# Two-block transformer kernel on one core: order and buffers of the modulation vectors in the first stages

## The reference, cut to what matters

```
h = rms_norm(x, g_mix)                       # x is 1024 tokens x 1024
z = h @ w_in                                 # iq (256), ik (64), iw (4), cx, cy (512 each), gt (3*1024), ...
q_i = rope(iq)   # 4 heads of 64;   k_i = rope(rms_norm(ik, g_idx_k))
w_i = iw * (IDX_HEADS ** -0.5 * IDX_DIM ** -0.5)
dots  = einsum('bqhe,bse->bqhs', q_i, k_i)   # per block of 128 queries
score = einsum('bqhs,bqh->bqs', relu(dots), w_i)
_, idx = lax.top_k(score, 256)               # which keys the second branch may see
gates = sigmoid(gt + b_gate)
# second block, once for each of its two layers and two conditions
mod = silu(cond) @ w_ada + b_ada             # w_ada is 1024 x 3072: shift, scale, gate
```

## Time and profile before

| | |
|---|---|
| median of three runs | 4141.89 us |
| the profiled execution's own time | 4143.85 us |
| its span | 4142.0 us |
| TensorE matmul busy | 3646.8 us (88%) |
| VectorE busy | 2171.8 us (52%) |
| ScalarE busy | 1415.1 us (34%) |
| mean DMA rate | 56 GB/s |

### The profile page before, as it was taken

One profiled execution on the slowest core, in us unless ns is written; L12 is line 12 of the kernel. 1 busy time (PEld: TensorE's weight loads), 2 busy tenths in 40 slices (PEclk: granted clock), 3 DMA queues, 4 the chain that ended last, 5 costly groups with the idle time before them and its releaser, 6 DMA issues. The chain is left out here.

```text
span 4142.0 us, 46440 instructions
## 1 busy us (share of the span) xinstructions
PE 3646.8 (88%) x19222; PEld 3017.1 (73%) x19222; DVE 2171.8 (52%) x3943; ACT 1415.1 (34%) x2519; POOL 238.0 (6%) x343
## 2 busy tenths in 40 slices
PE   7999988886999999999898788888698888888788
PEld 5888866765778888788666576776586777776667
DVE  4599934555733322323555545555535656425563
ACT  3211344444122211112344434444424445424341
POOL 2012110000100000000000000000000000000000
PEclk9799999887999999999899998988798999989999
DMA  3223330002421111111210001000211000100112
GB/s 122 83 104 126 117 108 27 21 21 81 163 82 46 46 38 51 53 47 36 87 34 23 29 26 32 26 27 22 91 61 65 31 30 30 36 20 18 32 33 95
DMA packets 69572, 230.08 MB, mean 56 GB/s; under 512 B 8745, under 2 KB 12841, under 8 KB 69361
## 3 DMA queue, kind: packets, MB, share of 16 engines
q1 hardware_dynamic: 43056, 132.68, 9.8%
q0 software_dynamic: 22848, 81.85, 5.8%
q10 hardware_dynamic: 3456, 12.58, 0.8%
HBM read 180.42 MB, written 36.17 MB: 52 GB/s over the span
## 5 line engine op out<-in xcount | busy, mean ns | idle before, releaser
L2388 PE MATMUL PS<-m,m 128*128 128x512 f32 (+3 forms) x3560 | 1419.7, 400 | 151.1 <-DVE m L2737 35.3
L2390 PE MATMUL PS<-m,m 128*128 128x512 f32 (+3 forms) x3560 | 1380.0, 389 | 0.0
L2389 PE MATMUL PS<-m,m 128*128 128x512 f32 (+3 forms) x3560 | 1379.3, 389 | 0.0
L2388 PEld LDWEIGHTS PS<-m,m 128*128 128x128 f32 (+2 forms) x3560 | 688.9, 194 | 327.5 <-issue 65.4
L2390 PEld LDWEIGHTS PS<-m,m 128*128 128x128 f32 (+2 forms) x3560 | 688.6, 194 | 137.7 <-issue 1.2
L2389 PEld LDWEIGHTS PS<-m,m 128*128 128x128 f32 (+2 forms) x3560 | 692.0, 195 | 120.2 <-issue 2.1
L2734 DVE TENSOR_TENSOR m<-m,m 128x1024 fp32r<-128x1024 f32 (+5 forms) x204 | 211.7, 1038 | 422.0 <-ACT m L2572 421.3
L3020 DVE TENSOR_TENSOR m<-PS,m 128x512 fp32r<-128x512 f32 x352 | 240.9, 689 | 295.3 <-ACT m L2664 295.0
L2664 ACT CAST m<-PS 128x512 fp32r<-128x512 f32 x352 | 205.4, 589 | 495.1 <-PE PS L2494 493.8
L2485 PE MATMUL PS<-m,m 64*128 64x256 f32 (+5 forms) x1968 | 254.1, 369 | 70.3 <-ACT m L2653 53.8
L2485 PEld LDWEIGHTS PS<-m,m 64*128 64x128 f32 (+1 forms) x1968 | 214.9, 199 | 115.0 <-ACT m L2653 69.0
(11 more groups left out here) (196 smaller groups left out, 3894.4 us busy)
## 6 DMA issues: line engine op xcount, KB each, us to landing
m<-in_w SPq DMA_DIRECT2D x220, 512.0 KB, 3.5
g_scratch<-m ACTq DMA_DIRECT2D x24, 512.0 KB, 2.6
m<-g_scratch POOLq DMA_DIRECT2D x24, 512.0 KB, 4.5
m<-in_w SPq DMA_DIRECT2D x32, 256.0 KB, 2.5
x_scratch<-m POOLq DMA_DIRECT2D x2, 4096.0 KB, 12.9
m<-m POOLq DMA_DIRECT2D x60, 128.0 KB, 2.7
m<-in_xT POOLq DMA_DIRECT2D x24, 256.0 KB, 7.4
y_scratch<-m POOLq DMA_DIRECT2D x12, 512.0 KB, 3.0
```

The source lines that it names most:

```text
L2388: pe.e.engine.matmul(o, L[0], X[0], start=start, stop=False)
L2389: pe.e.engine.matmul(o, L[0], X[1], start=False, stop=False)
L2390: return pe.e.engine.matmul(o, L[1], X[0], start=False, stop=stop)
```

## The change

Five things are written in another order, and nothing is added to or taken from the arithmetic.

- In `ik` two modulations stand instead of three, each behind three k-steps.
- The column sums of the second norm come two k-steps before the end of `iq0`'s first half, and their spreading after two k-steps of `iq1` instead of four, so that six k-steps of `iq1` stand behind it.
- The loads of weight tiles 3 and 4 (`cx0`, `cy0`) are issued before the first modulations' loads. They were issued behind the first five of those.
- From the second norm's end on the ring has four buffers instead of two: the two of the beginning and two further ones, and within the scores four others that lie over temporary buffers no longer in use. In the gate stage it has two again. There are four signals instead of two.
- Between `iq1` and the scores stand eight modulations instead of five, and twelve between the scores instead of eight, one behind every second head. The last six gates (18 to 23) have none. The total stays 48.

```diff
-MOVES, GATE_STORES, RING = 12, 4, 2
+MOVES, GATE_STORES, RING = 12, 4, 4
...
+    def m_use(slots, upto, after=()):
+
+        n = len(m_slots)
+        m_ring.update(slots=slots, start=n, upto=min(upto, 48), after=list(after))
+        m_fetch(n + len(slots))
+
+    def m_fetch(upto):
+        slots, start = m_ring["slots"], m_ring["start"]
+        while len(m_slots) < min(upto, m_ring["upto"]):
...
+            m_slots.append(slots[(n - start) % len(slots)])
+            free = m_ring["after"] + [(S.mod, m_all[n - RING])] * (n >= RING) if n - start < len(slots) else [
+                (S.mod, m_all[n - len(slots)])]
...
-    m_fetch(RING, [t_x[7, 0]])
+    w_load(5)
+    m_use(first_ring, 2, [t_x[7, 0]])
...
-            for _ in range(3):
-                steps_of(ik, 2)
+            for _ in range(2):
+                steps_of(ik, 3)
                 modulate()
             steps_of(ik, 2)
-            steps_of(q0, 8)
+            steps_of(q0, 6)
             next(second)
-            steps_of(q1, 4)
+            steps_of(q0, 2)
+            steps_of(q1, 2)
             finish(second)
             normed = [t for k in range(8) for t in h_ready[k, 512]]
-            steps_of(q1, 4)
+            m_use(first_ring + side_ring, 16, normed)
+            steps_of(q1, 6)
...
             modulate()
+            modulate()
             k_t = end("k", 0) + end("k", 1)
...
+            modulate()
             begin("q1", 1)
             modulate()
             modulate()
             end("q0", 1)
-            modulate(last=True)
             end("q1", 1)
-            modulate(last=True)
-            ring = late_ring
-            m_fetch(m_next[0] + RING, normed + [(S.mod, m_all[m_next[0] - 1])])
+            modulate()
+            modulate()
+            modulate()
+            gone = [t for i in range(4) for t in pairs_free[i]]
+            with mem.over(tmp_at):
+                late_ring = [mem([P, T]) for _ in range(4)]
...
-                    if nr % 3 == 0:
-                        modulate(nr > 18)
+                    if nr % 2 == 0:
+                        modulate()
+                    if nr == 6:
+                        m_use(late_ring, 22, gone)
...
-                    if n == 7:
+                    if n == 7 and m_next[0] < 48:
                         modulate()
```

More of the change, by code:

```diff
@@ L1195, in schedule, with modulate @@
         wlo.append(mem([P, 1024], R))
-        ring = [mem([P, T]) for _ in range(RING)]
+        first_ring = [mem([P, T]) for _ in range(2)]
     m_bank = {"ev": 6, "od": 7}
     m_all = [(kind, m_) for kind in ("ev", "od") for m_ in range(24)]
[L1199 to L1203, removed]
+    m_slots, m_ring = [], {}
+    m_next = [0]
+    def m_use(slots, upto, after=()):
[5 more added lines that the diff above has]
+        while len(m_slots) < min(upto, m_ring["upto"]):
+            n = len(m_slots)
             kind, m_ = m_all[n]
             at_ = W_AT[f"{kind[0]}a{m_}"][0]
[L1206 to L1210, removed]
+            m_slots.append(slots[(n - start) % len(slots)])
+            free = m_ring["after"] + [(S.mod, m_all[n - RING])] * (n >= RING) if n - start < len(slots) else [
+                (S.mod, m_all[n - len(slots)])]
+            p.add("eload", n=n, out=m_slots[n][:, :], in_=w[at_:at_ + P * 1024].rearrange("(p c) -> p c", p=P),
+                  signal=S.ring[n % RING], free=free)
+    def modulate():
         n = m_next[0]
         m_next[0] += 1
+        ring = m_slots[n]
         kind, m_ = m_all[n]
         at_ = 512 * m_bank[kind] + 2 * m_
-        p.add("mod", of=kind, m=m_, L=[ring[n % RING][:, 128 * k:128 * k + 128] for k in range(8)],
+        p.add("mod", of=kind, m=m_, L=[ring[:, 128 * k:128 * k + 128] for k in range(8)],
               o=PS[:, at_:at_ + 2], csil=csil, after=(S.ring[n % RING], ("ea", n)))
-        if not last:
-            m_fetch(n + 1 + RING)
+        m_fetch(n + 1 + len(m_ring["slots"]))
     def first_norm(c, sums=None):
@@ L1251, in schedule @@
             ikh, ikl = mem([P, T], R), mem([P, T], R)
+            tmp_at = mem.at
             tmp = [mem([P, 512]) for _ in range(8)]
@@ L1254, in schedule @@
             wi = mem([P, 8, 4])
-            late_ring = [mem([P, T]) for _ in range(RING)]
+            side_ring = [mem([P, T]) for _ in range(2)]
             late_end = mem.at
@@ L1334, in schedule @@
             finish(ik)
-            w_load(4)
             w_prep(4)
@@ L1341, in schedule @@
             finish(q0)
-            w_load(5)
             w_prep(5)
@@ L1414, in schedule @@
             u, i_, a_, th = (mem([P, T]) for _ in range(4))
-            ring = [mem([P, T]) for _ in range(RING)]
-            m_fetch(m_next[0] + RING, [(S.mod, m_all[m_next[0] - 1])])
+            m_use([mem([P, T]) for _ in range(2)], 48, [(S.mod, m_all[21])])
             xc_t, gl_t = [], []
```

## The result

The changed kernel takes 4163.42 us (4156.79 to 4172.2, six runs) against 4137.39 us of the kernel before in the same session: a ratio of 1.0065, 95% interval 1.0049 to 1.008. It is slower, by 26 us, inside the range that was given and 8 us above the forecast. The forecast had started from a median of 4141.89, though: the rise itself is 26.0 us where 13.9 was forecast. The profiled execution took 4171.52 us (span 4169.7).

A forecast was written before the change was run, and what follows sets the result against it. TensorE, busy nearly without a gap from the scores on, was taken as the bound, at a varying clock. The terms -5.1 + 8.0 + 14.1 + 0.5 - 3.6 gave +13.9 us, hence 4155.8 us, range 4139 to 4165.

The forecast's parts named there:

- First norm and `ik`, roots sooner: Up to the end of `iq1`: one modulation fewer, earlier clock rise and second norm's roots sooner save 5.1 us.
- Before the scores: From `iq1` to the first score: eight modulations, transfer waits gone, clock falling after two; +8.0 us.
- Between the scores: First score to last one's end: twelve pairs of heads and eleven slow modulations of 3.51 us; +14.1 us.
- at most two thirds: In the scores: a pair of heads takes at most two thirds of a group of three, 30.3 us for twelve.
- The longest pair: In the scores: the longest pair of heads takes under 3.4 us, so the clock was expected low all through.
- Behind the scores: After the last score: two heads end close together, so relu and sum come some 0.5 us later.
- The last gates: Gates 18 to 23: of 10.7 us of modulations removed, only those in gates 20 and 23 move the end; -3.6 us.
- upper end of 4165: Whole kernel: top of the range in us, from 30.3 us of scores and the clock falling at once.
- The lower end: Whole kernel: bottom of the range, 4139 us, from the low ends of `ik` and of the gates together.
- The first rival: Before and in the scores: transfer waits, not modulations, lower the clock, so it holds; -28 us, 4114; chance 0.12.
- The second: Last gates: waits hang on TensorE, so removed modulations pay 10.7 us instead of 3.6; +6.8 us, 4148.7; chance 0.12.
- The third: `ik` and scores: clock rises as often as before, two of eleven modulations fast; +5.0 us, 4146.9; chance 0.12.

The follow-up runs named there:

- roots: Kernel before with only the second norm's column sums and their spreading moved ahead; 4138.48 us, ratio 0.9997 to before.
- scores8: Changed kernel with eight modulations between the scores, one behind every third head, the four others in gates 18 to 21; 4137.67 us, ratio 1.0002 to before.
- gates6: Kernel before with the six modulations of gates 18 to 23 moved behind `cx` and `cy`, two in a row there; 4155.57 us, ratio 1.0032.
- rings: Kernel before with only the four buffers and the earlier loads of two weight tiles, modulations unmoved; 4136.25 us, ratio 0.9991.
- fours: Changed kernel with its twelve score modulations placed two behind every fourth head instead of one behind every second; 4139.88 us, ratio 1.0011 to before.
- late: Changed kernel without modulations from the end of `ik`'s first half to the last score; 46 stand singly behind `cx`, `cy` and in gates; 4107.25 us, ratio 0.9931 to before.
- pre2: `late` with two modulations put behind the end of `iq1` and two fewer in the gates; 4107.0 us, ratio 0.9936 to before.

## Why the prediction was right, and which term was off

The sign, the mechanism and the place were right. By its own steps:

- **First norm and `ik`, roots sooner: -5.1 forecast, -0.02 in the first profile, -8.9 in the second.** The roots gave their 1.4 us at the rotation (63.58 against 65.19 together with `ik`) and no more at the end of `iq1`, as `roots` shows. I had followed the gain to the rotation and taken it as the end's. For `ik` the range was given with the moment of the clock's rise, and both ends occurred, and beyond: the rise came later than before in one execution and at the first chance in the other.
- **Before the scores: +8.0 forecast, +6.85 measured.** The waits went and the clock fell, after three modulations instead of two.
- **Between the scores: +14.1 forecast, +21.1 measured. This is the term that was mis-sized.** Modulations and clock were as forecast (eleven at 3.51 us, 0.50 throughout). The pairs of heads took 33.6 us, not 26.6, and more than the 30.3 that I called the upper bound. The step that was off is "at most two thirds" of a group of three: it counts the heads' work and leaves out that a head of more than 512 columns starts alone. Up to 512 columns the pairs took 1.26 to 1.60 us, near the forecast. Of 640 columns, three heads had taken 4.16 us in the kernel before and a pair took 3.13, three quarters, at 1.2 GHz both times. In the timelines of TensorE, before and after:

```profile
131.70 0.79 PE L2388 MATMUL PS<-m,m 64*128 64x512 f32 x1
...
135.86 3.57 PE L2464 MATMUL PS<-m,m 128*128 128x2 f32 x16
```

```profile
139.45 0.79 PE L2405 MATMUL PS<-m,m 64*128 64x512 f32 x1
...
142.58 3.57 PE L2481 MATMUL PS<-m,m 128*128 128x2 f32 x16
```

  The longest pair was 3.88 us, not under 3.4. `scores8` shows the other side: with three heads together, and the clock back for some of them, they took 3.8 us less.
- **Behind the scores: +0.5 forecast, +0.15 measured.**
- **The last gates: -3.6 forecast, -2.52 measured, -2.73 alone in `gates6`.** The waits for GpSimd grew as argued. In the summary of the waits, which answers to the earlier trace rows:

```profile
PE PS L2405 <- POOL m L3146: 15.1, 4, 4.9
```

15.1 us instead of 7.7, so 7.4 of the 10.7 us came back as waiting; the four waits grew by 1.8 to 2.0 us each.

The terms sum to +25.9 us up to the gates' fence, against +13.9; of the 12.0 us between, 7.0 are the scores and 5.1 the beginning, with opposite small ones besides.

That the time still lay in the range is in part luck. It is 1.6 us below the upper end of 4165, and what that end was said to be made of, 30.3 us of scores and the clock falling at once, adds 3.7 and 3.6 us and gives 4163.1, less than the 4163.42 measured. The lower end does not follow either: the low ends of `ik` and of the gates together give 4145.1, not 4139. The mechanism, the low clock all through the scores, was no luck: the traces of both sessions show it.

The medians say +26.0 in the first session and a ratio of 1.005 (some 20 us) in the second. That runs of one kernel spread over 15 us would fit the two beginnings, 9 us apart; only profiled executions show the clock, so this is not shown.

The first rival (the clock holds if nothing waits for transfers) is refuted three times: by the changed kernel, by `rings`, and by `gates6`, where the clock fell with no wait near. The second (the gates give all) is refuted by the 2.52 of 10.7 us. The third, that the clock rises as often as before, holds for `fours` and not for the change. The Trainium skill (TensorE: Matmul & The Clock Gate, "HAM oscillation — how this bites in real kernels") says that idle gaps between groups of matmuls bring the clock down, and its case is waits for transfers. The trace of `late` agrees, with a wait for VectorE: 5.3 us at 0.50 after 7.32 us of waiting. It is not the whole of it here: modulations bring the clock down as well, in `gates6` with TensorE busy for 100 of 100 us. What in them does it, the two columns or the 128 x 128 weights that are loaded for them, no run here tells apart.

## What to carry to other kernels

Price filler work at the clock that it leaves behind, not at its own length: the modulations of 3.5 us in the scores also made 21.9 us of scores into 33.6, while the same ones, one at a time in a long run of wide matmuls, cost 1.8 us each and nothing more. When an engine that is always busy runs at half speed, ask which of its instructions are small, take them out of the short stages altogether, and put them singly where wide work runs between them (4.7 us was the least in these runs), or into a wait. And follow a gained microsecond to the next place where the clock changes before counting it.

## What the hardware showed that was not expected

- Two modulations in a row lowered the clock in the middle of unbroken projections, three times of six (0.39 to 0.63 us a matmul at 201.18 in `gates6`, clock 0.93 over 100 us); single ones with 4.7 us of projections or more between them never did in `late`, from the first ones behind the scores to the recurrent branch.
- The same instructions began with `iq1` ending at 85.19 or 94.11 us. In one the clock rose before the modulation at 29.15, in the other near 44.5, so the moment is not fixed by the program alone.
- Two heads of more than 512 columns on the two halves of the array overlapped only from the second's start, 1.03 us after the first's; a pair took 3.88 us at 1.2 GHz.
- The scores began at 0.50 for 5.3 us in `late` and for 5.7 in `pre2`, whether the gap before them held two modulations and 3.50 us of waiting or 7.32 us of waiting alone.
